# Turned tokens written to PSUM with a step, read without one; the second pair's norm ahead of the parameters' copy

## The reference, cut to what matters

```python
def rms_norm(x, g):
    x32 = x.astype(jnp.float32)
    y = x32 * lax.rsqrt(jnp.mean(x32 * x32, axis=-1, keepdims=True) + RMS_EPS)
    return (y * g.astype(jnp.float32)).astype(x.dtype)
...
h = rms_norm(x, norm_mix[l])
proj = h @ w_in[l]
q_na, k_na, v_na, u_s5, q_xa, gate_logits = jnp.split(proj, IN_SPLITS, axis=-1)
```

## Time and profile before

| | us |
|---|---|
| median of 3 runs (636.17 to 636.45) | 636.39 |
| the profiled execution, its own time | 636.35 |
| its span, first to last instruction | 634.4 |
| PE busy | 590.0 (93%) |
| DVE busy | 422.1 (67%) |
| ACT busy | 325.8 (51%) |
| POOL busy | 214.5 (34%) |

### The profile page before, as it was taken

The page is one execution under the profiler, slowest core; times in us unless marked ns, Lnnn a source line. Parts: engine busy times, 40 slices in busy tenths (PEclk is TensorE's granted clock), DMA queues, the critical chain, the costliest instruction groups (busy, mean ns, idle before and its releaser), DMA issues.

```text
span 634.4 us, 9095 instructions
## 1 busy us (share of the span) xinstructions
PE 590.0 (93%) x3190; PEld 472.8 (75%) x3190; DVE 422.1 (67%) x779; ACT 325.8 (51%) x537; POOL 214.5 (34%) x234
## 2 busy tenths in 40 slices
PE   2899999999999999999999999998886999999892
PEld 1687788889777767777777888886565888888771
DVE  3978513694386573554743379436886899999867
ACT  4957332221345424454243336224476899899753
POOL 3416996994000900000000000030654543556610
PEclk9999999999999999999999999999999999999997
DMA  9994625320262222122322326973799999999544
GB/s 295 194 203 127 134 67 143 92 67 1 72 188 73 67 68 75 59 68 66 100 67 66 101 99 162 339 267 133 232 307 410 375 384 386 384 390 375 123 107 172
DMA packets 89233, 111.62 MB, mean 176 GB/s; under 512 B 19613, under 2 KB 66879, under 8 KB 89192
## 3 DMA queue, kind: packets, MB, share of 16 engines
q1 hardware_dynamic: 79128, 93.65, 45.5%
q0 software_dynamic: 7280, 15.25, 9.1%
q10 hardware_dynamic: 2784, 2.18, 1.3%
HBM read 102.08 MB, written 14.75 MB: 184 GB/s over the span
## 4 chain that ended last, share of the span: by engine, by line
PE 75%; DVE 9%; DMA 5%; issue 4%; POOL 3%; ACT 3%; SPq 1%; DVEq 0%; POOLq 0%; ACTq 0%
PE bank L1612 20%; PE bank L1614 20%; PE bank L1613 20%; DMA xg<-h_scratch,idx 3%; PE bank L1793 2%; PE bank L1767 2%; PE bank L1780 2%; PE bank L1996 2%; DVE w_lo L1004 2%; DVE h_lo L1030 1%; DMA tok_scratch<-pay,rowi 1%; PE bank L1728 1%; PE bank L1905 1%; POOL tok_scratch L2285 1%; PE bank L1732 1%
## 5 line engine op out<-in xcount | busy, mean ns | idle before, releaser
L1004 DVE TENSOR_TENSOR w_lo<-raw,w_hi 128x1024 fp32r<-128x1024 f32 x55 | 72.7, 1321 | 106.8 <-ACT w_hi L575 106.2
L1612 PE MATMUL bank<-h_hi,w_hi 128*128 128x512 f32 x320 | 128.7, 402 | 2.3 <-DVE w_lo L1004 1.7
L1614 PE MATMUL bank<-h_hi,w_lo 128*128 128x512 f32 x320 | 125.0, 390 | 0.0
L1613 PE MATMUL bank<-h_lo,w_hi 128*128 128x512 f32 x320 | 124.6, 389 | 0.0
L1484 DVE TENSOR_TENSOR e_lo<-eraw,e_hi 128x2048 fp32r<-128x2048 f32 x47 | 106.6, 2294 | 7.4 <-ACT e_hi L814 7.4
L814 ACT CAST e_hi<-eraw 128x2048 fp32r<-128x2048 f32 x48 | 91.9, 1918 | 9.0 <-PE bank L1614 9.0
L575 ACT CAST w_hi<-raw 128x1024 fp32r<-128x1024 f32 x55 | 57.5, 1045 | 33.8 <-PE bank L1614 33.6
L1612 PEld LDWEIGHTS bank<-h_hi,w_hi 128*128 128x128 f32 x320 | 60.1, 188 | 16.4 <-DVE w_lo L1004 2.4
L1614 PEld LDWEIGHTS bank<-h_hi,w_lo 128*128 128x128 f32 x320 | 60.0, 188 | 13.1
L1613 PEld LDWEIGHTS bank<-h_lo,w_hi 128*128 128x128 f32 x320 | 60.2, 188 | 11.3
L2238 POOL TENSOR_TENSOR wcf<-wcf,prt 128x160 f32<-128x160 f32 x1 | 0.5, 456 | 195.1 <-DMA wcf<-in_moe_w_fine 195.1
(11 more groups left out here) (401 smaller groups left out, 1241.9 us busy)
## 6 DMA issues: line engine op xcount, KB each, us to landing
raw<-in_w_in SPq DMA_DIRECT2D x40, 512.0 KB, 3.8
eraw<-in_moe_w_gate SPq DMA_DIRECT2D x32, 512.0 KB, 8.8
eraw<-in_moe_w_up SPq DMA_DIRECT2D x32, 512.0 KB, 13.6
eraw<-in_moe_w_down SPq DMA_DIRECT2D x32, 512.0 KB, 12.9
raw<-in_w_out SPq DMA_DIRECT2D x8, 512.0 KB, 3.8
x_sb<-in_x SPq DMA_DIRECT2D x4, 512.0 KB, 5.1
raw<-in_w_mem_kv SPq DMA_DIRECT2D x4, 512.0 KB, 8.7
raw<-in_w_br_na SPq DMA_DIRECT2D x4, 512.0 KB, 3.4
```

The source lines that it names most:

```text
L1004: dve.tensor_tensor(v(l_, o, [1, 1024]), v(raw, 1024 * (c % RAW), [1, 1024]), raw32(v(h_, o, [1, 1024])), SUB).then_inc(sem("w_lo_done"), 1)
L1612: pe.matmul(dst, w[0], x[0], start=first, stop=False)
L1613: pe.matmul(dst, w[0], x[1], start=False, stop=False)
L1614: return pe.matmul(dst, w[1], x[0], start=False, stop=last)
```

## The change

PE's transposes of x write each block's tokens to the column that they have in the product (step of 8 elements within PSUM), and ACT and DVE read and write without a step. Block 6 turns into bank 1 and block 7 into bank 4; block 7 alone waits, for `turn_lo` 1. DVE scales the second pair of tiles ahead of the wait for the parameters and their copy, and PE's order follows: block 6 of the first pair and block 0 of the second come ahead of the parameters. The transposes of `mem_sb` stay as they were.

```diff
-    TURN_BANK = (4, 5, 6, 7, 2, 3, 4, 5) + 2 * (4, 5, 6, 7)
+    TURN_BANK = (4, 5, 6, 7, 2, 3, 1, 4) + 2 * (4, 5, 6, 7)
...
             act.wait_ge(sem("turned"), b + 1)
             if b < KD:
-                act.activation(v(h_hi, SEQ * b, [1, ROWS], [ROWS, GW]), pv(TURN_BANK[b], 0, [GW, ROWS], [1, GW]),
-                               ACT.Identity, scale=pcol(GMIX + b)).then_inc(sem("turn_hi"), 1)
+                act.activation(v(h_hi, SEQ * b, [1, SEQ]), pv(TURN_BANK[b], 0, [1, SEQ]), ACT.Identity, scale=pcol(GMIX + b)).then_inc(sem("turn_hi"), 1)
...
         inverse_root(1, 0, 2)
         norm_x(0)
         norm_x(1)
+        inverse_root(2, 2, 2)
+        norm_x(2)
+        norm_x(3)
         dve.wait_ge(sem("prm_in"), 16 * 8)
         done(dve.tensor_copy(v(prm, 0, [64, 2], [1, 64], p0=LDT, pn=DP),
                              v(stat, 60, [1, 2], [0, 64], p0=LDT, pn=DP)), "prm_ready")
-        inverse_root(2, 2, 2)
-        norm_x(2)
-        norm_x(3)
         dve.wait_ge(sem("prm_turned"), 1)
         done(dve.tensor_copy(v(prt, 0, [1, 98]), pv(0, 0, [1, 98])), "prm_ready")
         def turn_lo(b):
             dve.wait_ge(sem("turn_hi"), b + 1)
             if b < KD:
-                o = [[1, ROWS], [ROWS, GW]]
-                dve.scalar_tensor_tensor(v(h_lo, SEQ * b, *o), pv(TURN_BANK[b], 0, [GW, ROWS], [1, GW]),
-                                         pcol(GMIX + b), raw32(v(h_hi, SEQ * b, *o)), MUL, SUB).then_inc(
+                dve.scalar_tensor_tensor(v(h_lo, SEQ * b, [1, SEQ]), pv(TURN_BANK[b], 0, [1, SEQ]),
+                                         pcol(GMIX + b), raw32(v(h_hi, SEQ * b, [1, SEQ])), MUL, SUB).then_inc(
                                              sem("turn_lo"), 1)
...
             if b < KD:
                 pe.wait_ge(sem("normed"), tiles[-1] + 1)
-                if b >= 6:
-                    pe.wait_ge(sem("turn_lo"), b - 5)
+                if b == 7:
+                    pe.wait_ge(sem("turn_lo"), 1)
...
             for n in tiles:
                 src = v(x_sb, D * n + P * b, [1, P]) if b < KD else v(mem_sb, D * n + P * (b - KD), [1, P])
-                ins = pe.transpose(pv(TURN_BANK[b], P * n, [1, P]), src, v(ident, 0, [1, P]))
+                o = pv(TURN_BANK[b], 2 * n, [1, 2], [ROWS, GW]) if b < KD else pv(TURN_BANK[b], P * n, [1, P])
+                ins = pe.transpose(o, src, v(ident, 0, [1, P]))
...
         for b in range(6):
             turn(b, (0, 1))
+        turn(6, (0, 1))
+        turn(0, (2, 3))
         turn_params()
-        for b in range(6):
+        for b in range(1, 7):
             turn(b, (2, 3))
-        for b in range(6, KD):
-            turn(b, (0, 1, 2, 3))
+        turn(7, (0, 1, 2, 3))
```

## The result

| | before, us | after, us |
|---|---|---|
| median (8 runs of each) | 636.27 | 631.20 |
| range of the runs | 634.47 to 636.71 | 630.25 to 633.93 |
| the profiled execution | 636.35 | 630.6 |
| its span | 634.4 | 628.6 |
| start of product 1 | 27.61 | 22.23 |

The ratio is 0.9923, with a 95% interval of 0.9909 to 0.9937. The changed kernel is faster by 0.8%, and in this pair of profiles everything is won ahead of product 1: 5.38 us there, and the rest of the span is 0.4 us shorter. That rest is no fixed number: over the twelve profiles of this case it goes from 605.7 to 608.9 us.

The account below looks back on a forecast made before the run. The start was taken as bound by DVE up to product 1, then PE. Reordering (1.95 us) plus h_lo's faster rate, cut off by PE's own work, gave 4.8: 636.4 - 4.8 = 631.6 us, range 630.8 to 634.6.

Parts of the forecast that it names:

- DVE's order: Second pair's norm, begun ahead of the parameters, ends at 13.04 us against 15.29; reordering alone gains 1.95 us.
- PE up to the parameters: Fourteen transposes fit inside the norm's wait; `prt` copied from 14.00, lo(0) from 14.29, h_lo(0) at 15.42 against 17.37 us.
- The step: Without the SBUF step h_lo takes 0.69 us, one every 0.60 instead of 1.13; ACT's 1242 ns becomes about 689.
- The stepped write into PSUM: PE's transposes writing PSUM with a step cost nothing; rival that it doubles a transpose: 637.9 us, chance 0.15.
- PE's clock: Rises three microseconds after PE resumes at 13.1 us, or still at 18.4; spread of -0.6 and +0.4 on 4.8 us.
- No stall: PE's transposes reach block 7 at 16.34 us, with h_lo(0) done at about 16.2, so PE does not wait.
- The rival that the clock rises only under product 0: Transposes do not raise PE's clock, product 0 runs three microseconds at half rate, losing 1.5 us: 633.1; chance 0.07.
- What comes along: POOL's 16 transfers and later chunks move up; the chunk landing at about 45.3 us, cast at 50.2, keeps 4.9 of cover.
- The rival of a part given back at the transfers: Earlier bias transfers make chunk 7 late, or parameters land after 13.0 us; up to 3.0 of 4.8 lost: 634.0; chance 0.08.

Follow-up runs that it names:

- The order alone: Changed kernel's order, banks and waits, with the steps back in ACT's and DVE's SBUF writes; 634.99 us, ratio 0.999 against the kernel before.
- the step alone: Kernel before's order, banks and waits; only the step moved from the SBUF writes to the transposes' PSUM writes; 633.95 us, ratio 0.9967.
- stepped pairs: Changed kernel with products 0 and 1 written to PSUM in pairs of values 64 bytes apart, ACT reading straight through; 631.22 us, one run.
- two experiments: The 0.42 us wait of chunk 5's cast is from no step anywhere; the text does not say which run has 0.76 us.
- no step anywhere: Changed kernel with transposes writing PSUM without a step, the tokens' reordering left out; 631.15 us, ratio 0.9923 against the kernel before.
- the same program again: The changed kernel's same file, nothing changed, profiled again with six runs; 631.85 us, ratio 0.9934 against the kernel before.
- the bias held: Changed kernel with POOL holding its 16 bias transfers until w_lo of chunk 2 is written; 631.54 us, ratio 0.9928 against the kernel before.
- the banks of before: Changed kernel with the old banks, blocks 6 and 7 waiting for h_lo(0) and h_lo(1); 632.65 us, ratio 0.9944 against the kernel before.
- the chunks ahead: Changed kernel with SP issuing chunks 4 and 5 right behind chunk 3, ahead of small loads; 632.08 us, ratio 0.9934 against the kernel before.

## Why the prediction was right, point by point

The forecast was 631.6 and the median is 631.2. By its own steps:

- **DVE's order: right.** The norm was to end at 13.04 and ended at 12.96. The parameters had landed by 12.99, as their copy shows no wait. The order alone gave 2.14 us of product 1's start, where 1.95 was written.
- **PE up to the parameters: right.** `prt` 14.00 written, 13.98 measured; lo(0) 14.29 and 14.28; h_lo(0) 15.42 and 15.42.
- **The step: right, with the pitch a tenth low.** h_lo 0.69 written, 0.740 measured; 0.66 apart, the upper of the two values given and not the 0.60 that the sum used. It cost nothing, since DVE was done at 21.9 with w_lo of chunk 1, ahead of 22.23. The order alone kept 1229 ns and the step alone had 744, so it is the step in SBUF that made the low part slow. Whether its write or the equally stepped read of h_hi does it isn't shown; `s_lo`, which the prediction took for a measure of the write, reads `s_hi` with its step too. For ACT, which had the write alone, it is the write.
- **The stepped write into PSUM: right.** It is free for these transposes. The Trainium skill, in Advanced Engine Details and Errata, PSUM Cachelines, spoke against it; by that rule a loss was to be feared. No run here agrees: 0.215 us apart at the lower level of the clock and four in 0.63 at the higher, with the step and without it, and stepped pairs at 0.227 under the products.
- **PE's clock: the term that was mis-sized.** It was to rise three microseconds after PE resumed, at about 16. In the profiled run it rose at 14.0, one microsecond after, so block 7 was reached at 15.3 and not 16.34. "No stall" was therefore wrong: PE waited 0.99 us for h_lo(0), and its four transposes ran at full rate. Product 0 started at 16.69, not at 17.2, and with blocks 0.69 apart product 1 started at 22.23, not 22.8. That is the 0.6 us between 5.38 and 4.8, a little more than the +0.4 that was written for it. The rival that the clock rises only under product 0 fell for this kernel, but came true in the step alone, and it nearly did in two kernels with the same start as this one, where the clock rose as product 0 began. That the clock rose early in the profile compared here is luck.
- **What comes along: incomplete.** Only the chunk with the latest landing was looked at, chunk 7, and it was right (44.2 against 45.3, cast at 49.49). The one that lost its cover is chunk 5. The table has issue, landing and ACT's cast of each of the four, worked out from the issue's row and its time to landing; none of these casts waits for its chunk:

| | before: issued, landed, cast | cover | after: issued, landed, cast | cover |
|---|---|---|---|---|
| chunk 4 | 22.71, 27.3, 40.26 | 13.0 | 21.84, 31.8, 34.74 | 2.9 |
| chunk 5 | 24.36, 31.5, 46.59 | 15.1 | 25.03, 40.6, 41.07 | 0.4 |
| chunk 6 | 24.84, 35.2, 52.75 | 17.6 | 25.51, 42.4, 47.23 | 4.8 |
| chunk 7 | 27.58, 45.3, 55.01 | 9.7 | 28.64, 44.2, 49.49 | 5.3 |

The bias transfers began at 19.77 and not 25.01, ahead of chunk 5, whose landing went from 7.1 to 15.6 us while its cast came 5.5 us earlier. The rival of a part given back at the transfers didn't come about in the changed kernel by 0.4 us. It is real from there on, as the 0.42 and 0.76 us of two experiments show.

Where the time is compared to 0.3 us nothing is settled: the start of one and the same program differs by 0.64 us between two profiles, and the runs of the changed kernel reach over 3.7 us. The two profiles also differ far behind the change: PE's waits for gathered tokens in the mixture of experts were 8.8 us before and 6.7 after, with nothing changed there. Against that, PE lost about 2.5 us after, and none before, to a fall of its clock at 471 us, shown below. So the rest of the span came out at 606.4, close to the forecast 606.8, with two differences of over 2 us in it that nearly cancel: that is in part luck.

## What to carry to other kernels

When data has to be permuted on its way through PSUM, look at which of its writers is cheapest to burden: here the transpose took the step for nothing, while two engines each paid 0.5 us a tile for it in SBUF. When a start is moved forward, list every transfer whose trigger moves with it and every load that is issued behind those, with landing and first use, since the one to run out of cover need not be the one that lands last. Sum a gain only up to where the next engine takes over: of the 8 x 0.47 = 3.8 us by which h_lo got faster, PE let 3.2 through.

## What the runs showed of the hardware that wasn't expected

**When PE's clock rises.** The granted clock reads 1.00 over 10 to 20 us in every profile here, as in this row of the changed kernel (busy time and count of each engine, then clock, DMA share and GB/s):

```profile
10.00:20.00 10.00, 8.65 (x47) 7.48 (x46) 8.43 (x17) 7.46 (x14) 0.23 (x1) 1.00 1.08 277
```

The pitch of the transposes shows the real level: 0.215 us, then about 0.11. The trace's own list of clock stretches explains the difference: it begins at 14.0 us in the changed kernel and at 18.7 before, where the pitch halves, and holds nothing ahead of that. By both, transposes alone bring PE from the level of 1.2 GHz to that of 2.4, ahead of any product, in eight of the twelve profiles of this case; in three it rose as product 0 began, and in the step alone over a microsecond later. The Trainium skill, in TensorE: Matmul & The Clock Gate, PE-mode transpose, says that they don't; these rows disagree. The moment varies with little cause: 12.3 us with no step anywhere, 14.0 in the changed kernel, 14.6 in the same program again, 17.5 with the bias held, 18.4 with the banks of before, 20.7 with the step alone. PE had idled 0.64 us ahead of the second pair with the bias held and 0.36 in the changed kernel, but not at all in the same program again, so this idle time alone doesn't order them, and what sets the moment stays open. Between 14.0 and 17.5 lie 0.7 us of product 1's start, of which 0.26 is a later norm.

**When it falls again.** In the mixture of experts PE waits for gathered tokens. These are the eight transposes behind one such wait, before and after, and the stretch around them after:

```profile
477.47 1.16 PE L1996 MATMUL bank<-ident,xg 128*128 128x128 f32 x8 [2.75 <-DMA xg<-h_scratch,idx]
```

```profile
472.47 1.97 PE L1996 MATMUL bank<-ident,xg 128*128 128x128 f32 x8 [3.10 <-DMA xg<-h_scratch,idx]
```

```profile
471.00:479.00 8.00, 6.53 (x21) 5.54 (x22) 4.02 (x5) 3.96 (x5) 2.94 (x5) 0.57 1.03 413
```

After the wait of 2.75 us the clock stayed at 1.00, and with the one of 3.10 us it fell. The length of the wait alone does not decide: the kernel before has one of 2.82 us at 491 without a fall, and the banks of before one of 2.64 at 486 with a fall. The eight transposes then took 1.97 and not 1.16 us, and nine matmuls stood 0.43 and not 0.23 apart, about 2.5 us in all. Eight of the twelve profiles have such a fall at 471 to 492 us, for 3.4 or 6.8 us each, and the kernel before, the order alone, the chunks ahead and the bias held have none. It is one reason why the rest of the span varies by microseconds between programs that don't differ there.

**A step of 32 bytes in SBUF** costs ACT 1242 against 704 ns, in its write alone, and DVE 1230 against 740, in its write and one of its reads, for 128 x 512 fp32 values out of PSUM, a factor of 1.8 and 1.7. ACT's read of PSUM with a step of 64 values costs nothing: the copy to uT takes 588 ns in the changed kernel and 589 in the kernel with stepped pairs, where it reads straight through.

**Small transfers ahead of a large one.** Sixteen bias transfers of some 61 KB each, issued from another queue, made a 512 KB load take 15.6 us where it takes 5.5 with them issued behind it.
